# Four 64x64 inverses of a hybrid trunk: x and z signalled apart, and banks shared out anew

## The reference, cut to what matters

```python
a_mat = jnp.where(strict, jnp.einsum('bhnid,bhnjd->bhnij', kb, kc) * dmat, 0.0)
rhs = jnp.concatenate([vc * bc[..., None], kb * jnp.exp(gc)[..., None]], axis=-1)
sol = lax.linalg.triangular_solve(a_mat + jnp.eye(l, dtype=jnp.float32), rhs,
                                  left_side=True, lower=True, unit_diagonal=True)
...
def step(s, inp):
    q_i, qk_i, u_i, w_i, k_i, gl = inp
    v_new = u_i - jnp.einsum('bhck,bhkv->bhcv', w_i, s)
    o = jnp.einsum('bhck,bhkv->bhcv', q_i, s) + jnp.einsum('bhij,bhjv->bhiv', qk_i, v_new)
    s = s * gl[..., None, None] + jnp.einsum('bhck,bhcv->bhkv', k_i, v_new)
```

## Time and profile before

| what | value |
|---|---|
| median of 3 runs | 1686.23 us (1684.91 to 1686.81) |
| the profiled execution's own time | 1688.43 us |
| its span in the profile | 1686.6 us |
| busy share of PE, DVE, ACT, POOL | 97%, 61%, 50%, 14% |
| granted TensorE clock, mean | 0.99 of full speed |

### The profile page before, as it was taken

One profiled execution on the slowest core, in us unless ns is written; L12 is line 12 of the kernel. 1 busy time (PEld: TensorE's weight loads), 2 busy tenths in 40 slices (PEclk: granted clock), 3 DMA queues, 4 the chain that ended last, 5 costly groups with the idle time before them and its releaser, 6 DMA issues.

```text
span 1686.6 us, 40072 instructions
## 1 busy us (share of the span) xinstructions
PE 1633.1 (97%) x17501; PEld 1550.6 (92%) x17501; DVE 1030.0 (61%) x1688; ACT 837.4 (50%) x1599; POOL 240.3 (14%) x293
## 2 busy tenths in 40 slices
PE   7999999999999999999999999999999999999997
PEld 6999899999897899997788987999999998899997
DVE  6965677754556877444372356776448936777654
ACT  4754466643545666431532225665336645666533
POOL 6005340000110200002003230200010016310000
PEclk9999999999999999999999999999999999999999
DMA  7941335555653555652534001455557521455550
GB/s 213 275 151 40 114 122 179 189 194 187 213 166 125 173 184 182 200 175 63 179 104 132 10 4 58 140 188 197 179 157 235 185 83 40 135 187 176 199 175 27
DMA packets 244963, 250.27 MB, mean 148 GB/s; under 512 B 15936, under 2 KB 238686, under 8 KB 244702
## 3 DMA queue, kind: packets, MB, share of 16 engines
q1 hardware_dynamic: 237040, 224.74, 42.3%
q0 software_dynamic: 7440, 22.86, 4.6%
q10 hardware_dynamic: 308, 0.10, 0.0%
HBM read 229.75 MB, written 18.32 MB: 147 GB/s over the span
## 4 chain that ended last, share of the span: by engine, by line
PE 91%; DVE 4%; ACT 3%; issue 1%; DMA 0%; SPq 0%; DVEq 0%
PE ps L745 89%; PE ps L749 2%; DVE tri L2460 1%; ACT acts L1861 1%; DVE acts L2468 1%; DVE hn L2468 0%; ACT hn L1861 0%; DVE acts L2460 0%; DVE st L2468 0%; DVE st L2460 0%; DMA acts<-in_x_sample_dram 0%; ACT w_mlstm L1861 0%; ACT w_gdn L1861 0%; PE ps L1632 0%; DVE acts L2464 0%
## 5 line engine op out<-in xcount | busy, mean ns | idle before, releaser
L2460 DVE TENSOR_TENSOR w_mlp<-ring,w_mlp 128x1024 fp32r<-128x1024 f32 x256 | 311.8, 1225 | 121.7 <-ACT w_mlp L1861 115.6
L1861 ACT ACTIVATE w_mlp<-ring 128x1024 fp32r<-128x1024 f32 x256 | 269.4, 1054 | 211.6 <-PE ps L745 211.6
L745 PE MATMUL ps<-hn_split,w_mlp 128*128 128x264 f32 x3072 | 373.3, 284 | 0.0
L745 PE MATMUL ps<-h_split,w_mlp 128*128 128x264 f32 x3072 | 372.6, 284 | 0.0
L745 PEld LDWEIGHTS ps<-hn_split,w_mlp 128*128 128x128 f32 x3072 | 372.1, 188 | 0.3
L745 PEld LDWEIGHTS ps<-h_split,w_mlp 128*128 128x128 f32 x3072 | 371.7, 188 | 0.0
L745 PE MATMUL ps<-gdn_hi,w_gdn 128*128 128x264 f32 x1024 | 195.9, 291 | 7.0 <-DVE mixer_lo L2460 7.0
L1861 ACT ACTIVATE tri<-ps 128x264 f32<-128x264 f32 (+4 forms) x184 | 80.9, 442 | 201.8 <-PE ps L745 200.4
L745 PEld LDWEIGHTS ps<-gdn_hi,w_gdn 128*128 128x128 f32 x1024 | 163.7, 192 | 10.2 <-issue 8.9
L1861 ACT ACTIVATE acts<-ps 128x264 f32<-128x264 f32 (+4 forms) x126 | 56.3, 451 | 199.7 <-PE ps L745 198.3
L745 PE MATMUL ps<-mixer_lo,w_gdn 128*128 128x264 f32 x512 | 147.3, 288 | 0.0
(11 more groups left out here) (406 smaller groups left out, 2322.9 us busy)
## 6 DMA issues: line engine op xcount, KB each, us to landing
ring<-in_ffn_w_dram SPq DMA_DIRECT2D x128, 1024.0 KB, 5.4
ring<-in_gdn_w_in_dram SPq DMA_DIRECT2D x32, 1024.0 KB, 6.0
ring<-in_ml_w_in_dram SPq DMA_DIRECT2D x12, 1024.0 KB, 5.5
ring<-in_rw_w_rkv_dram SPq DMA_DIRECT2D x12, 1024.0 KB, 5.2
st<-in_state_gdn_S_dram POOLq DMA_DIRECT2D x2, 4096.0 KB, 23.0
ring<-in_gdn_w_out_dram SPq DMA_DIRECT2D x8, 1024.0 KB, 5.0
out_gdn_S_s_dram<-st SPq DMA_DIRECT2D x16, 512.0 KB, 3.9
st<-in_state_mlstm_C_dram POOLq DMA_DIRECT2D x1, 4096.0 KB, 20.0
```

What stands on the lines that cost most here:

```text
L745: return nc.tensor.matmul(out, lhsT, rhs, start=start, stop=stop)
L1861: return nc.scalar.activation(out, in_, f, bias=bias, scale=scale)
L2460: return nc.vector.tensor_tensor(out, in0, in1, op)
```

## The change

DVE signals x and z apart: x's subtraction gives `x_ev` and z's gives `Q_ev`. On a level DVE subtracts both halves of x first, each behind its wait for `Q_mm`, and then both halves of z. On level 0 it forms both halves of z ahead of x. PE's product waits for `x_ev` instead of `Q_ev`, and Q waits for `Q_ev` besides `P_ev`. The update of x is written to the bank of the product, 0 or 1 (ACT has copied it out by then), and the update of z to bank 2 or 3, so an inverse has banks 0 to 3. The fills move to banks 4 to 7: `OUTER`, `spread_queries` (now in banks 4 and 5 by turns, before in 2 to 5) and `first_fill` (now in 4 to 7, before in 6 and 7). `x_ev` is another name for a semaphore that an unrelated part of the program also uses.

```diff
-        OUTER = ((0, (2, 1), 3, 5), (4, (3, 1), 3, 5), (1, (4, 1), 3, 5), (5, (5, 0), 6, 3), (2, (5, 2), 7, 2), (6, (5, 3), 6, 3),
+        OUTER = ((0, (2, 1), 4, 5), (4, (3, 1), 4, 5), (1, (4, 1), 4, 5), (5, (5, 0), 6, 7), (2, (5, 2), 4, 5), (6, (5, 3), 6, 7),
                  (3, None, 4, 5), (7, None, 2, 3))
...
+        x_ev = kd_ok
...
                         if l:
-                            pe.wait_ge(Q_ev, count.seen(Q_ev))
+                            pe.wait_ge(x_ev, count.seen(x_ev))
...
-                        last_read[b] = P_ev if l else Q_ev, count.expect(P_ev if l else Q_ev)
+                        last_read[b] = (P_ev, count.expect(P_ev)) if l else (x_ev, count.expect(x_ev))
...
                         pe.wait_ge(P_ev, count.seen(P_ev))
-                        b, bt = 2 + h, 4 + h
-                        if l < LEVELS64 - 1:
-                            pe.wait_ge(*last_read[b])
-                        pe.wait_ge(*last_read[bt])
+                        pe.wait_ge(Q_ev, count.seen(Q_ev))
+                        b, bz = h, 2 + h
+                        pe.wait_ge(*last_read[b])
+                        pe.wait_ge(*last_read[bz])
...
                 def spread_queries():
                     for q in range(4):
-                        b = 2 + q
+                        b = 4 + q % 2
...
                 def first_fill(n):
-                    b = 6 + n % 2
+                    b = 4 + n % 4
...
             def invert64(fill, x_, m_, z_):
 
-                for l in range(LEVELS64):
+                for h in range(2):
+                    eight = slice(8 * h, 8 * h + 8)
+                    dv.wait_ge(lm_ok, count.seen(lm_ok))
+                    tt(z_[:, eight, :], bc(ids[:], 8, 1), m_[:, eight, :], ALU.subtract).then_inc(Q_ev, count.up(Q_ev))
+                for h in range(2):
+                    eight = slice(8 * h, 8 * h + 8)
+                    dv.wait_ge(P_mm, count.seen(P_mm))
+                    tt(x_[:, eight, :], bc(ids[:], 8, 1), mats8(h), ALU.subtract).then_inc(x_ev, count.up(x_ev))
+                    if (0, h) in fill:
+                        fill[0, h]()
+                count.seen(lm_ok, 2 * LEVELS64 - 2)
+                for l in range(1, LEVELS64):
...
                         dv.wait_ge(Q_mm, count.seen(Q_mm))
                         if l < LEVELS64 - 1:
-                            tt(x_[:, eight, :], x_[:, eight, :], mats8(2 + h), ALU.subtract)
-                        tt(z_[:, eight, :], z_[:, eight, :], mats8(4 + h), ALU.subtract).then_inc(Q_ev, count.up(Q_ev))
+                            tt(x_[:, eight, :], x_[:, eight, :], mats8(h), ALU.subtract).then_inc(x_ev, count.up(x_ev))
+                    for h in range(2):
+                        eight = slice(8 * h, 8 * h + 8)
+                        tt(z_[:, eight, :], z_[:, eight, :], mats8(2 + h), ALU.subtract).then_inc(Q_ev, count.up(Q_ev))
                         if (l, 2 + h) in fill:
                             fill[l, 2 + h]()
```

More of the change, by code:

```diff
@@ L891, in invert64 @@
                             for r in halves:
-                                last = mm(ps[bt][r, at], px_[r, m, :], z_[r, m, :])
+                                last = mm(ps[bz][r, at], px_[r, m, :], z_[r, m, :])
                         last.then_inc(Q_mm, count.up(Q_mm))
-                        last_read[bt] = Q_ev, count.expect(Q_ev)
                         if l < LEVELS64 - 1:
-                            last_read[b] = last_read[bt]
+                            last_read[b] = x_ev, count.expect(x_ev)
+                        last_read[bz] = Q_ev, count.expect(Q_ev)
                         if (l, 2 + h) in fill:
@@ L2043, in gdn @@
                     ac.wait_ge(qe_mm, count.seen(qe_mm))
-                    act(QS[:, 2 * q:2 * q + 2, :], ps[2 + q][:].rearrange("p (n t) -> p n t", n=2), ACT.Exp).then_inc(
+                    act(QS[:, 2 * q:2 * q + 2, :], ps[4 + q % 2][:].rearrange("p (n t) -> p n t", n=2), ACT.Exp).then_inc(
                         eq_ev, count.up(eq_ev))
@@ L2580, in invert64 @@
             def invert64(fill, x_, m_, z_):
-                for l in range(LEVELS64):
+                for h in range(2):
[10 more added lines that the diff above has]
+                for l in range(1, LEVELS64):
                     for h in range(2):
-                        if l and (l, h) in fill:
+                        if (l, h) in fill:
                             fill[l, h]()
```

## The result

The changed kernel takes 1709.64 us, the median of four executions (1708.38 to 1712.71), against 1685.57 (1682.2 to 1686.81): a ratio of 1.0145 with a 95% interval of 1.0122 to 1.0169. It is slower by 24 us where 10 were forecast. Of the executions behind the experiments two of e7 (1801 and 7256 us), one of e8 (1848) and one of the kernel before (2303) were disturbed, and medians, ranges and ratios leave them out.

A forecast was written before the change was run, and what follows sets the result against it. PE, busy 97% of the span, was taken as the bound. Each GDN layer adds 1.80+3.13+0.2, two layers +10.2, RWKV 0.0; on the median's scale 1696.4 us, range 1692.5 to 1701.0.

The forecast's parts named there:

- levels 0.60 each: GDN levels 2, 3, 4: key transposes wait for later keys, +0.60 a level, +1.80 a layer.
- level 5 with the wait for the keys in bank 7: GDN level 5: outer(3)'s second matmul waits for keys until 188.94 instead of 187.14, +1.80, within +3.13 a layer.
- z0 behind both Q: GDN level 5: z0 moves from 190.50 to 194.05 and solve_values(0) waits for it; within +3.13 a layer.
- the gram: First RWKV inverse: the fill behind P(1,0), now in bank 4, waits for ACT to empty it, +0.85.
- the boundary: Between the RWKV inverses: z ahead of x on level 0 brings mask and bonus products earlier, net -1.85.
- the end: End of the second RWKV inverse: z1 waits for the last product and z0, +0.54.
- C: GDN levels: transposes wait only for PE's own order, not keys, so levels win time; 1689.1, chance 0.10.
- D: Product of each level: x's early signal is what counts, a gain of 4.4; 1681.8, chance 0.03.
- E: GDN level 5: new waits fall under other work, levels 2 to 4 cost as forecast; 1689.4, chance 0.07.
- rival B: GDN inverses: forecast waits plus one or two more 1.2 GHz stretches of 1.6 each; 1698.0 or 1699.6, chance 0.18.
- RWKV's levels: Second RWKV inverse, levels 1 to 3: new_state behind x1 and z0 delays new sums by 0.16, +0.5 in all.
- K5: Theory of the experiments: idle time of GDN level 5 alone brings TensorE to 1.2 GHz for long; no chance given.

The follow-up runs named there:

- e7: e4 with the keys operations back behind z1; 1686.49 us, ratio 0.9987 to the kernel before.
- e8: The changed kernel with the edits of e2 and e3, levels 1 to 4 as changed; 1689.42 us, ratio 1.0011 to the kernel before.
- e1: The changed kernel, but on levels 1 to 4 DVE subtracts x and z of a half together again; 1703.06 us, ratio 1.0090.
- e2: The changed kernel with other banks for five outer products, from the one behind P(5,0) on; 1698.72 us, ratio 1.0063.
- e3: The changed kernel, but on level 5 DVE subtracts each half of z behind its own wait; 1698.93 us, ratio 1.0069.
- e10: e4 with each half of the product waiting for the same half of z too; 1695.40 us, ratio 1.0056.
- e9: e4 with spread_queries back in banks 2 to 5; 1682.14 us, ratio 0.9978.
- e6: The changed kernel with first_fill back in banks 6 and 7; 1707.72 us, ratio 1.0113.
- e5: The kernel before with outer(3)'s second matmul in bank 7 and the next outer product in 3 and 2; 1695.84 us, ratio 1.0047.
- e11: The kernel before with a wait for the keys added behind both matmuls of outer(3); 1687.31 us, ratio 1.0006.
- e12: e4 with outer(3) in banks 6 and 7 and the next outer product in 4 and 5; 1689.81 us, ratio 1.0031.
- e4: The changed kernel with DVE order x0, z0, x1, keys, z1, edits of e2 and e3, first_fill in banks 6 and 7; 1679.07 us, ratio 0.9965.

## Why the prediction was wrong

**What held.** The bottleneck, and the price of each GDN wait: levels 0.60 each (e1 takes exactly this away), level 5 with the wait for the keys in bank 7 (e2 takes it away), z0 behind both Q (e3), solve_keys for the adds. The two GDN layers at full clock cost 10.3 by the forecast's terms (2 x 5.13, which the text rounds to 10.2) and 10.3 by measurement. In RWKV the gram, the boundary and the end came within 0.2 of their terms. Rivals C and D fell: the transposes waited for keys, with 1.29 written in the row. E fell as well: outer(3) was late by 2.14 in the row, and solve_keys waited for an add.

**What failed.** The step "One more stretch at 1.2 GHz is 1.6, two are 3.2", rival B with a chance of 0.18. The mechanism was named, its size was not: the forecast put the clock at nothing, and the rival took the one stretch behind the first GDN inverse of before, 3.4 us long, as the unit, with no bound on how long a stretch lasts. The same trace has stretches twice that long elsewhere (435.6 to 442.5 and 1265 to 1272), as in this row of the kernel before:

```profile
1265.00:1272.00 7.00, 5.36 (x22) 5.25 (x23) 6.33 (x17) 4.28 (x9) 1.41 (x1) 0.51 0.83 250
```

The one that the waits of level 5 brought lasted 20.5 us in the second layer and 6.8 in the first, 7.8 and 1.6 of cost. The long stretch is not one accident of the profiled execution: the four executions of the changed kernel have mean clocks of 0.980 to 0.984, those of before 0.988 to 0.995; the stretch at the start of the profiled execution accounts for 0.003 of its 0.982. The range ended at 1701 because of this one term.

The Trainium skill, TensorE: Matmul & The Clock Gate, section "A second HAM failure mode: psum-queue depth-cycling", describes such a loss, for small idles between groups of matmuls that cycle through PSUM banks. The trace agrees for level 5, where an idle of 2.14 between small groups was followed by 1.2 GHz; it does not for levels 2 to 4, where idles of 1.29 and 1.85 changed little (e8, e10: no stretch over 3.4 us).

**A smaller miss.** For RWKV's levels +0.5 was forecast, 0.16 each from new_state, and 1.4 was measured. The rows of solved (`rw,tri`) on levels 3 and 4 of the second inverse, in the kernel before, e9 and e8:

```profile
998.51 0.58 PEld L745 LDWEIGHTS ps<-rw,tri 64*64 64x64 f32 x16
1007.84 0.58 PEld L745 LDWEIGHTS ps<-rw,tri 64*64 64x64 f32 x16
```

```profile
990.30 0.58 PEld L746 LDWEIGHTS ps<-rw,tri 64*64 64x64 f32 x16
999.63 0.58 PEld L746 LDWEIGHTS ps<-rw,tri 64*64 64x64 f32 x16
```

```profile
999.18 0.58 PEld L746 LDWEIGHTS ps<-rw,tri 64*64 64x64 f32 x16
1008.66 0.58 PEld L746 LDWEIGHTS ps<-rw,tri 64*64 64x64 f32 x16
```

From one such row to the next it is 8.86, 9.34 and 9.33 in the kernel before, and the same in e9, which has the split signal, z ahead of x on level 0 and x's update in bank 0 or 1, but DVE's old order on the levels. e8 has the new order and 9.01, 9.48 and 9.48: 0.15 a level, as forecast from new_state, which on levels 1 and 3 of the changed kernel ends 0.1 before new sums' loads start. The changed kernel has 9.01, 9.62 and 9.93, and 0.4 more on level 4. So 0.4 is new_state, and the other 1.0 are pauses of PE within its groups (0.18 at 1002.17, 0.36 at 1006.28, 0.33 at 1021.61) with no releaser named. The profiled executions of e1, e2, e6, e7 and e10 have such pauses too, those of before, e5, e8, e9, e11 and e12 have none there. What brings them stays open.

**What stays open.** What decides whether a wait on level 5 brings the lower clock. The inverses with a wait of 1.5 or more between the two matmuls of outer(3) (the changed kernel, e1, e3, e5, e6) had a stretch of 17 us or more in six of ten profiled layers, and e12, with 0.94 and 1.52, one of 10 in one layer of two. Those with less (before, e2, e4, e7, e8, e9, e11) had none over 6.8 in fourteen. e10, with 1.49 ahead of P(5,1) instead, had none over 3.4, and e11's 1.02 is too short to tell place from length. So K5 holds as "level 5, not the levels before", and fails as "a wait of that length anywhere in level 5". Place, length and what PE does around it were not taken apart further.

## What to carry to other kernels

Price a wait on TensorE twice: once by its length, and once by what the clock does behind it; where a trace has one slow stretch, its length is no bound for the next. An earlier signal pays only if the operation queued behind it is ready too: here the split signal was worth nothing in a GDN level until the keys went ahead of z1 (e7), and 13 to 16 us in all then (e10). And banks that fills share with what a slower engine empties are waits: two entries of a table cost 8 to 10 us (e5).

## What was not expected of the hardware

A wait of 1.54 us on TensorE was followed by 17 us at 1.2 GHz (e5, clock 0.51 from 190 to 207), and the edit that brought it cost 8 to 10 us in all, while waits of 1.85, 1.85 and 1.49 in e10's first layer left it at 2.4 GHz. In the six layers with a stretch of 17 us or more the lower level began within 3 us behind the wait, and in e5 it lasted through a stretch in which PE was busy 96% of the time.
